# Sample rows' projection: high and low halves side by side in one stationary operand, two products per step instead of three

## The reference, cut to what matters

```python
h = rmsnorm(x, lp['norm_g']) * (1 + scale[:, None]) + shift[:, None]
proj = h @ lp['w_in']
```

## Time and profile before

| what | value |
| --- | --- |
| three runs | 2047.07, 2050.80, 2051.19 us (median 2050.8) |
| profiled execution, span from first to last instruction | 2045.6 us |
| mean granted TensorE clock of the core | 0.899 of full speed |
| PE, PEld, DVE, ACT, POOL busy | 91%, 65%, 52%, 31%, 6% of the span |
| data moved by DMA | 230.58 MB, mean 113 GB/s |

### The profile page before, as it was taken

One profiled execution on the slowest core, in us unless ns is written; L12 is line 12 of the kernel. 1 busy time (PEld: TensorE's weight loads), 2 busy tenths in 40 slices (PEclk: granted clock), 3 DMA queues, 4 the chain that ended last, 5 costly groups with the idle time before them and its releaser, 6 DMA issues. The chain is left out here.

```text
span 2045.6 us, 23911 instructions
## 1 busy us (share of the span) xinstructions
PE 1867.0 (91%) x8467; PEld 1329.9 (65%) x8499; DVE 1056.1 (52%) x2098; ACT 637.8 (31%) x1154; POOL 126.4 (6%) x218
## 2 busy tenths in 40 slices
PE   6699999999999999983999896799999997978998
PEld 1587877877887788741655793344445445976886
DVE  0367646954875487451356565455555535414332
ACT  3325434344343423240321361233333331202100
POOL 3111110000000000000130000000000002000000
PEclk9699999999999999996799655899999996558999
DMA  7537565444544466442521001010100004204441
GB/s 251 169 123 232 186 207 216 154 161 144 216 170 155 145 184 216 155 160 81 167 80 43 25 19 47 11 32 11 32 11 26 1 1 113 74 1 161 135 142 53
DMA packets 145092, 230.58 MB, mean 113 GB/s; under 512 B 14486, under 2 KB 98103, under 8 KB 144502
## 3 DMA queue, kind: packets, MB, share of 16 engines
q1 hardware_dynamic: 117475, 162.03, 24.6%
q0 software_dynamic: 15920, 53.55, 7.2%
q10 hardware_dynamic: 11579, 13.48, 2.2%
HBM read 175.27 MB, written 56.15 MB: 113 GB/s over the span
## 5 line engine op out<-in xcount | busy, mean ns | idle before, releaser
L649 PE MATMUL ps<-h_hi,w_hi 128*128 128x512 f32 x832 | 341.4, 410 | 1.1 <-DVE c_u L999 1.1
L651 PE MATMUL ps<-h_lo,w_hi 128*128 128x512 f32 x832 | 325.7, 391 | 0.0
L650 PE MATMUL ps<-h_hi,w_lo 128*128 128x512 f32 x832 | 325.2, 391 | 0.0
L2239 PE MATMUL ps<-pT,values 128*65 128x512 f32 x412 | 217.1, 610 | 1.0
L2301 ACT ACTIVATE pT<-ps 128x512 f32<-128x512 f32 x206 | 123.0, 597 | 295.4 <-PE ps L2226 195.7
L2381 DVE TENSOR_REDUCE part_max<-ps 128x1 f32<-128x512 f32 (+3 forms) x272 | 143.1, 558 | 123.3 <-PE ps L2254 49.2
L1030 DVE SCALAR_TENSOR_TENSOR c_acc<-c_u,par,c_acc 128x512 f32<-128x512 f32 x240 | 180.1, 751 | 6.8
L649 PEld LDWEIGHTS ps<-h_hi,w_hi 128*128 128x128 f32 x832 | 157.3, 189 | 37.2 <-issue 6.0
L650 PEld LDWEIGHTS ps<-h_hi,w_lo 128*128 128x128 f32 x832 | 157.4, 189 | 35.9 <-issue 6.0
L651 PEld LDWEIGHTS ps<-h_lo,w_hi 128*128 128x128 f32 x832 | 156.8, 188 | 34.1
L1468 PE MATMUL ps<-raw,x_in 128*128 128x254 f32 (+1 forms) x320 | 137.7, 590 | 0.0
(11 more groups left out here) (615 smaller groups left out, 3102.1 us busy)
## 6 DMA issues: line engine op xcount, KB each, us to landing
w_hi<-split_weights SPq DMA_DIRECT2D x78, 512.0 KB, 3.6
w_lo<-split_weights SPq DMA_DIRECT2D x78, 512.0 KB, 4.5
w_raw<-in_w_in SPq DMA_DIRECT2D x26, 512.0 KB, 4.6
split_weights<-w_hi POOLq DMA_DIRECT2D x26, 512.0 KB, 5.6
split_weights<-w_lo POOLq DMA_DIRECT2D x26, 512.0 KB, 6.3
x_in<-in_x_prompt SPq DMA_DIRECT2D x4, 2048.0 KB, 10.9
tm<-in_x_prompt SPq DMA_DIRECT2D x16, 512.0 KB, 4.4
out_y_prompt<-y_out SPq DMA_DIRECT2D x16, 512.0 KB, 2.9
```

Source lines behind the costliest of these rows:

```text
L649: m.matmul(out, w_hi[:, b, kk, :], hh[:, kk, :], start=(kk == 0), stop=False)
L650: m.matmul(out, w_lo[:, b, kk, :], hh[:, kk, :], start=False, stop=False)
L651: return m.matmul(out, w_hi[:, b, kk, :], hl[:, kk, :], start=False, stop=(kk == KT - 1))
L2239: m.matmul(k.ps[0:VW, 5 + b, :], k.va[:, t, b, :], pT[:, i % NPT].rearrange("p h q -> p (h q)"), start=first, stop=end).then_inc(z["pv_don ...
```

## The change

The high and low halves of the sample rows are put in one tile `hs_both` of 40 columns per step: the high half in columns 0 to 7, the low half in columns 32 to 39, the 24 between set to zero once. A step then has two products, `hs_both` with the high weights and `hs_both` with the low ones. They write 40 partitions of the bank: partitions 0 to 7 hold hi·(hi+lo), partitions 32 to 39 hold lo·(hi+lo). DVE copies the first eight partitions to `srow` as before, and then adds partitions 32 to 39 to it; the add now frees the bank. The lo·lo product, which was left out before, is in the sum now.

```diff
@@ stage_trunk @@
+    HS_LOW, HSW = 32, 32 + NS
@@
-        hs32, hs_hi, hs_lo = sb("hs32", [P, KT, NS]), sb("hs_hi", [P, KT, NS], FR), sb("hs_lo", [P, KT, NS], FR)
+        hs32, hs_both = sb("hs32", [P, KT, NS]), sb("hs_both", [P, KT, HSW], FR)
+        hs_hi, hs_lo = hs_both[:, :, 0:NS], hs_both[:, :, HS_LOW:HSW]
@@ sample_rows @@
                 if u == "tm":
-                    hi, lo, out = wt_hi, wt_lo, k.ps[0:NS, b, 0:NTM]
+                    hi, lo, out = wt_hi, wt_lo, k.ps[0:HSW, b, 0:NTM]
...
-                    hi, lo, out = w_hi[:, i % NWB], w_lo[:, i % NWB], k.ps[0:NS, b, slot * P:(slot + 1) * P]
+                    hi, lo, out = w_hi[:, i % NWB], w_lo[:, i % NWB], k.ps[0:HSW, b, slot * P:(slot + 1) * P]
                 for kk in range(KT):
-                    m.matmul(out, hs_hi[:, kk, :], hi[:, kk, :], start=(kk == 0), stop=False)
-                    m.matmul(out, hs_hi[:, kk, :], lo[:, kk, :], start=False, stop=False)
-                    last = m.matmul(out, hs_lo[:, kk, :], hi[:, kk, :], start=False, stop=(kk == KT - 1))
+                    m.matmul(out, hs_both[:, kk, :], hi[:, kk, :], start=(kk == 0), stop=False)
+                    last = m.matmul(out, hs_both[:, kk, :], lo[:, kk, :], start=False, stop=(kk == KT - 1))
@@ scalar @@
-            a.copy(hs_hi[:, :, :], hs32[:, :, :]).then_inc(z["hs_a"], 1)
+            a.copy(hs_hi, hs32[:, :, :]).then_inc(z["hs_a"], 1)
@@ vector @@
             v.memset(pa[:, :, 0:2], 0.0)
+            v.memset(hs_both[:, :, NS:HS_LOW].bitcast(F32), 0.0)
             v.memset(ubuf[:, :, 0:PADC], 0.0).then_inc(z["zero"], 1)
...
-            v.tensor_tensor(hs_lo[:, :, :], hs32[:, :, :], hs_hi[:, :, :].bitcast(F32), ALU.subtract).then_inc(z["hs_v"], 1)
+            v.tensor_tensor(hs_lo, hs32[:, :, :], hs_hi.bitcast(F32), ALU.subtract).then_inc(z["hs_v"], 1)
@@ fill @@
-                    v.tensor_copy(srow[:, f % 2, 0:size], k.ps[0:NS, b, 0:size]).then_inc(bank_r[b], 1)
+                    link(v.tensor_copy(srow[:, f % 2, 0:size], k.ps[0:NS, b, 0:size]))
+                    v.tensor_tensor(srow[:, f % 2, 0:size], k.ps[HS_LOW:HSW, b, 0:size], srow[:, f % 2, 0:size], ALU.add).then_inc(bank_r[b], 1)
```

## The result

The changed kernel took 2033.8 us (median of nine runs, 2031.1 to 2042.7) against 2047.7 for the kernel before (median of nine, the three known ones among them). The ratio is 0.9939, 95% interval 0.9924 to 0.9954. Run again later with twelve runs of its own it took 2037.4 us, ratio 0.9958 (0.9944 to 0.9972). As a ratio the forecast was 0.9952. Two later runs of the kernel before, 2174 and 2951 us at mean clocks of 0.788 and 0.551, are left out throughout.

A forecast was written before the change was run, and what follows sets the result against it. TensorE was taken to bound the kernel, busy 91% of the span. Removed products 13.9 − new waits 1.5 − swallowed savings 0.96 − clock 1.56 = 9.9 us, off the median 2050.8: 2040.9 us, range 2036.0 to 2047.5.

The forecast's parts named there:

- Removed products: Eight of 24 sample products go per tile, 12.5 us over 26 tiles, plus 1.45 in `tm`: 13.9 us.
- The wider load: Sample products with 40 stationary columns keep 0.060 us each, since 64-column loads hide entirely at 0.055 a pass.
- load rivals: Loads in series: gain 2.0, 2048.8 us, chance 0.09. Loads setting the pace, slower: about 2065 us, chance 0.05.
- upper end of 0.13 us: Upper bound for a sample product with 40 columns, from 128-column loads: four in 0.52 us, 0.13 each.
- The second DVE operation: An add after each sample-row copy, at the copy's time: 5.0 us more of DVE, 1.5 us of new PE waits.
- two of its waits: PE waits on the bank about 0.4 us before `x2` and 1.0 us before `z0`.
- The third, 0.1 us at the transpose: After the fill following `q1`, the first transpose of the next group waits 0.1 us for the add.
- DVE did not pace the group: Rival: every add lands on the path, 5.0 instead of 1.5 us; gain 6.4, 2044.4 us; chance 0.09.
- Swallowed savings: PE's idle before `x4` grows from 2.47 to 2.95 us, before `q1` from 1.88 to 2.36; 0.96 us lost.
- The clock, 1.56 us: The idle of 2.36 us before `q1` brings a fall to the lower clock, counted as 1.56 us.
- I take the difference off the median: 2040.9: Whole kernel: the gain of 9.9 us is subtracted from the runs' median, 2050.8, rather than the profiled span, 2045.6.
- The range: Whole kernel: 2036.0 to 2047.5 us, taking in the forecast's span and the rival where DVE paces, 0.83.

The follow-up runs named there:

- run with zeros: The changed kernel with a third product per step whose stationary operand is 40 columns of zeros: 2060.5 us, ratio 1.0065.
- table of widths: The changed kernel with stationary operands of different width per tile, 8 to 128 columns, to read the spacing of products: 2055.3 us.

## Why the prediction was right or wrong

The step that failed is the base from which the gain was taken, and with it the range; the mechanism held.

- **Removed products, 13.9 us.** Right: 0.95 instead of 1.44 us a tile, 2.92 instead of 4.36 for the packed block, 0.060 a product. The run with zeros confirms it from the other side. Only the first block, `gs0`, ran at the lower clock and went from 2.52 to 1.70 us, 0.82 instead of 0.48.
- **The wider load.** Right, and by the reason given: 40 columns load in the shadow of the product. Both load rivals fell with the table of widths; the bend lies just above the 64 columns of the row that the argument used. The upper end of 0.13 us was misread: four loads in 0.52 us are three distances and a last load of 0.19, so 0.11 from start to start, which is what 128 columns then took.
- **The second DVE operation.** Its price (0.68 and 0.57 us) and two of its waits, idle 0.27 and 1.05 us, are as forecast, and without it they vanish. From start to start they cost 0.43 and, with the fall after `x4`, 1.26 us; without that fall the second costs 0.66. The third, 0.1 us at the transpose, did not show. DVE did not pace the group.
- **Swallowed savings.** Right: idle 2.93 and 2.36 us.
- **The clock, 1.56 us.** The fall after `q1` came in seven of nine profiles, and in the first the lead shrank by 1.6. The argument for it failed: 2.36 was counted because it is nearer to 2.47 than to 1.88, yet 2.8 to 2.9 us brought a fall in only four of the nine, and in the run with zeros the clock fell after 1.89. The term also counted one fall as a fixed cost where others come and go; in the first profile another one stayed away and gave 1.7 back. What the term is worth on average is not shown: 0.4 ± 0.8 us by the mean clocks. The gain of 10.7 ± 0.4 at equal clock is 0.7 below the sum without the term, 11.4.
- **"I take the difference off the median: 2040.9."** This is the failure that put the time outside the range. Of the 7.1 us between forecast and result, 5.6 lie in the base (2050.8 where the kernel before stands at 2045.2 at equal clock), 0.8 in the gain (9.9 where 10.7 was measured), and 0.7 in the nine runs of the changed kernel, whose median was that much under its level. The median of three was also 4.2 us above the median of the 54 later runs (2046.6); two of the three were high. The third, 2047.07, was the better base: all later runs lie 1.5 to 1.7 us above their span, so by its distance to the span of 2045.6 it is the profiled execution itself. It gives 2047.1 − 9.9 = 2037.2, or 2035.7 without the clock term, 1.9 us from the result. The 5.2 us between median and span were thus 1.5 around the span and 3.7 of chance.
- **The range.** Its lower end, 2036.0, left room for a gain of 14.8 below 2050.8 but for no error of the base beside it. As a ratio, 0.9952, the forecast lies at the upper end of the first interval and between the two measured. Which nine runs were drawn also mattered: the twelve later ones, median 2037.4, lie inside the range.

## What to carry to other kernels

Beside 128 moving columns a load of the stationary operand was free up to 64 columns here, so small operands can share one load; check from start to start, not by durations. Before arguing about a few microseconds, take the base of a forecast from the profiled run, and look at the clock of every run that you compare. When a tile grows, look where it pushes its neighbours: keep the large stationary tiles at the same place modulo 256 bytes, and compare the spacing of products that the edit does not touch, over the same stretch of work and not of time.

## What the runs showed of the hardware that was not expected

Thirty-two unused bytes in front of `w_hi` and `w_lo` made the main products of 128 by 128 with 512 moving columns 5.5 ns slower at full clock (233.2 instead of 227.7 ns), and the kernel 12.5 us slower at equal clock. The few main products at the lower clock kept their spacing of 0.426 to 0.427 us (25 pairs with the pad, 12 without). Products with 128 and 400 moving columns kept their 0.060 and 0.182 us; in them `w_hi` and `w_lo` are the moving side or have no part, so this doesn't tell whether the number of columns matters or the side. Of eight places tried, the three that are multiples of 256 bytes from the old one were quick, and the others not. Why was not found; multiples of 128 between them, and other absolute addresses, were not tried.

A full load of 128 float32r columns is no quicker than its width says: 0.109 us at 128 columns, on the line through 0.071 at 80 and 0.089 at 104.

An idle time of TensorE brings a clock fall in some runs and not in others: after 2.36 us in seven of nine profiles, after 2.8 to 2.9 us in four of the same nine.

The kernel's time follows its mean clock closely, 1.36 us for each 0.001 between 0.894 and 0.903. For the kernel before, the spread between runs shrinks from a standard deviation of 2.8 us to 1.6 when the clock is taken out, for the changed one from 4.1 to 1.9.
